# Running sums of the convolution taps of the third and fourth up stage in two free PSUM banks instead of SBUF

## The reference, cut to what matters

```python
def causal_dwconv(x, w, b=None):              # width 3 here
    y = sum(xp[:, j:j + t] * w[j] for j in range(width))
    return y if b is None else y + b

def conv_gated_mlp(hn, w_up, conv_w, conv_b, w_down):
    u = causal_dwconv(hn @ w_up, conv_w, conv_b)
    gate, val = jnp.split(u, 2, axis=-1)
    return (jax.nn.silu(gate) * val) @ w_down
```

## Time and profile before

| | us |
|---|---|
| three runs | 1355.68, 1353.02, 1345.2; median 1353.02 |
| the profiled execution | 1350.6, of which the span of the profile is 1348.8 |
| TensorE busy | 1277.2 (95%) |
| VectorE busy | 980.0 (73%) |
| ScalarE busy | 765.5 (57%) |
| GpSimd busy | 253.8 (19%) |

### The profile page before, as it was taken

The page is one execution under the profiler, slowest core; times in us unless marked ns, Lnnn a source line. Parts: engine busy times, 40 slices in busy tenths (PEclk is TensorE's granted clock), DMA queues, the critical chain, the costliest instruction groups (busy, mean ns, idle before and its releaser), DMA issues.

```text
span 1348.8 us, 28806 instructions
## 1 busy us (share of the span) xinstructions
PE 1277.2 (95%) x10587; PEld 1244.5 (92%) x10587; DVE 980.0 (73%) x1665; ACT 765.5 (57%) x1269; POOL 253.8 (19%) x233
## 2 busy tenths in 40 slices
PE   6999999999999999999968999999989998999997
PEld 6999999988999999988867999999989988999997
DVE  5766557876867755797799554789976786799954
ACT  5544445696554444579834554566665565666652
POOL 0000000010000000044406102345540021355500
PEclk9999999999999999999988999999999999999998
DMA  7555564563366656464527113865556523565563
GB/s 234 179 174 169 141 175 140 175 193 95 112 202 186 178 159 192 139 212 136 170 82 211 35 48 117 205 197 182 178 157 194 189 79 110 157 185 177 159 184 105
DMA packets 76733, 212.87 MB, mean 158 GB/s; under 512 B 7973, under 2 KB 22389, under 8 KB 76528
## 3 DMA queue, kind: packets, MB, share of 16 engines
q1 hardware_dynamic: 73536, 202.47, 49.3%
q0 software_dynamic: 2832, 9.04, 3.0%
q10 hardware_dynamic: 288, 0.33, 0.1%
HBM read 208.74 MB, written 3.06 MB: 157 GB/s over the span
## 4 chain that ended last, share of the span: by engine, by line
PE 61%; DVE 20%; issue 8%; DMA 4%; ACT 4%; POOL 2%; DVEq 1%; SPq 0%; ACTq 0%
PE bank L501 14%; PE bank L503 14%; PE bank L502 13%; DVE wl L394 4%; DVE cv L802 3%; DMA raw<-in_w_up 2%; DVE tp L782 2%; DVE cv L799 1%; PE bank L1549 1%; DVE sc L799 1%; DVE dVT L2219 1%; PE bank L2673 1%; PE bank L2763 1%; PE bank L1551 1%; DVE gTmp L2285 1%
## 5 line engine op out<-in xcount | busy, mean ns | idle before, releaser
L389 ACT ACTIVATE wh<-raw 128x1024 fp32r<-128x1024 f32 (+3 forms) x428 | 409.4, 963 | 312.3 <-PE bank L503 234.3
L394 DVE TENSOR_TENSOR wl<-raw,wh 128x1024 fp32r<-128x1024 f32 (+3 forms) x385 | 426.5, 1116 | 148.7 <-ACT wh L389 147.8
L501 PE MATMUL bank<-XH,wh 128*128 128x256 f32 (+1 forms) x1456 | 415.5, 285 | 13.5 <-DVE XL L890 7.0
L503 PE MATMUL bank<-XH,wl 128*128 128x256 f32 (+1 forms) x1456 | 413.0, 284 | 0.0
L502 PE MATMUL bank<-XL,wh 128*128 128x256 f32 (+1 forms) x1456 | 412.8, 284 | 0.0
L501 PEld LDWEIGHTS bank<-XH,wh 128*128 128x128 f32 x1456 | 275.6, 189 | 16.1 <-DVE XL L890 7.7
L503 PEld LDWEIGHTS bank<-XH,wl 128*128 128x128 f32 x1456 | 276.0, 190 | 0.0
L502 PEld LDWEIGHTS bank<-XL,wh 128*128 128x128 f32 x1456 | 274.7, 189 | 0.0
L501 PE MATMUL bank<-AH,wh 128*128 128x256 f32 (+1 forms) x704 | 199.0, 283 | 6.4 <-DVE wl L394 4.1
L394 POOL TENSOR_TENSOR wl<-raw,wh 128x1024 fp32r<-128x1024 f32 x43 | 113.3, 2637 | 480.0 <-ACT wh L389 479.8
L503 PE MATMUL bank<-AH,wl 128*128 128x256 f32 (+1 forms) x704 | 198.5, 282 | 0.0
(11 more groups left out here) (375 smaller groups left out, 2268.9 us busy)
## 6 DMA issues: line engine op xcount, KB each, us to landing
raw<-in_w_up SPq DMA_DIRECT2D x176, 512.0 KB, 4.3
raw<-in_w_down SPq DMA_DIRECT2D x64, 384.0 KB, 3.5
raw<-in_w_down SPq DMA_DIRECT2D x64, 320.0 KB, 3.1
raw<-in_w_gvz SPq DMA_DIRECT2D x32, 512.0 KB, 4.4
raw<-in_w_gqk SPq DMA_DIRECT2D x16, 512.0 KB, 5.1
raw<-in_w_gout SPq DMA_DIRECT2D x16, 512.0 KB, 4.5
raw<-in_w_mv SPq DMA_DIRECT2D x8, 512.0 KB, 5.0
raw<-in_w_mqk SPq DMA_DIRECT2D x8, 512.0 KB, 5.0
```

The costliest lines, as they stand in the source:

```text
L389: eng.activation(WH[s][:, 0:n, :], raw[s][:, 0:n, :], ACT.Copy).then_inc(s_hi[s], 1)
L394: eng.tensor_tensor(WL[s][:, 0:n, :], raw[s][:, 0:n, :], WH[s][:, 0:n, :].bitcast(F32), ALU.subtract).then_inc(s_lo[s], 1)
L501: eng.matmul(out, WH[s][:, i, :], xh, start=start, stop=False)
L503: mm = eng.matmul(out, WL[s][:, i, :], xh, start=False, stop=stop)
```

## The change

`tap2` and tap 1 write the running sum in a PSUM bank (bank 6 for even, bank 7 for odd units) and no longer in `dst`. Tap 0 reads the sum from the bank and writes the result to `dst` in SBUF, where `silu` and `prod` read it as before. The wait for the `silu` of the iteration before moves from ScalarE's `tap2` to VectorE's tap 0; for values a wait for the `prod` of the iteration before is added there. Both taps keep their numbers of elements, and no instruction is added or removed apart from the waits.

```diff
+            def sums(self, u):
+                return bank[6 + u % 2][:, 0:self.st.T]
+
             def tap2(self, eng, it, u):
                 m, T = it * 4 + u, self.st.T
                 evacuated(eng, self.st, it, u)
+                self.tap2s.done(eng.activation(self.sums(u), TP[u % 2][:, 3:3 + T], ACT.Identity,
+                                               bias=v(self.bias, m), scale=v(self.w, m + 88)), f"tap2_{u}")
+
+            def tap(self, eng, it, u):
+                m, T, acc = it * 4 + u, self.st.T, self.sums(u)
+                self.tap2s.wait(eng, it, f"tap2_{u}")
+                self.taps.done(eng.scalar_tensor_tensor(acc, TP[u % 2][:, 2:2 + T], v(self.w, m + 44), acc, ALU.mult,
+                                                        ALU.add), f"tap1_{u}")
+                self.taps.wait(eng, it, f"tap1_{u}")
                 if u % 2 == 0:
                     self.silus.wait(eng, it, f"silu{u // 2}", back=1)
-                self.tap2s.done(eng.activation(self.dst(u), TP[u % 2][:, 3:3 + T], ACT.Identity,
-                                               bias=v(self.bias, m), scale=v(self.w, m + 88)), f"tap2_{u}")
-
-            def tap(self, eng, it, u):
-                m, T, dst = it * 4 + u, self.st.T, self.dst(u)
-                self.tap2s.wait(eng, it, f"tap2_{u}")
-                self.taps.done(eng.scalar_tensor_tensor(dst, TP[u % 2][:, 2:2 + T], v(self.w, m + 44), dst, ALU.mult,
-                                                        ALU.add), f"tap1_{u}")
-                self.taps.wait(eng, it, f"tap1_{u}")
-                self.taps.done(eng.scalar_tensor_tensor(dst, TP[u % 2][:, 1:1 + T], v(self.w, m), dst, ALU.mult,
+                else:
+                    self.prods.wait(eng, it, f"prod{u // 2}", back=1)
+                self.taps.done(eng.scalar_tensor_tensor(self.dst(u), TP[u % 2][:, 1:1 + T], v(self.w, m), acc, ALU.mult,
                                                         ALU.add), f"tap0_{u}")
```

## The result

| | us |
|---|---|
| before, 14 runs | median 1351.63 (1342.14 to 1355.68) |
| after, 14 runs | median 1343.37 (1335.99 to 1349.8) |
| ratio after to before | 0.9945, 95% interval 0.9928 to 0.9963 |
| span of the profile | 1348.8 before, 1340.6 after |

The change makes the kernel 0.55% faster: 7.4 us by the ratio, 8.2 between the two spans. The forecast was 8.4.

A forecast was written before the change was run, and what follows sets the result against it. TensorE was taken to bound up4's middle and VectorE, by little, up3's. 1.5 + 2.59 + (2.52 - 0.1) + (2.07 - 0.1) = 8.5, taken as 8.4: 1353.0 - 8.4 = 1344.6 us, range 1337 to 1351.

The forecast's parts named there:

- Bounds: Middles of the up stages: VectorE bounds up3 by little, its period 0.16 us above TensorE's; TensorE bounds up4.
- Reading and writing PSUM: VectorE's taps: reading a bank is free, writing one taken as 0.48 us per tap, bounds 0.47 and 1.07.
- The exclusion: Taps with two SBUF inputs stand until GpSimd is done; with one, 2.40, 0.63 and 0.74 us fall to 0.48.
- VectorE per iteration: Up stage loop: 8.83 us of VectorE work, 9.2 with 0.1 for each wait, against TensorE's 11.37.
- Middle of up3: Up3's 33 units return to TensorE's pace, 95.25 to 93.75 us: 1.5 back.
- First gap: Between up3's last matmul and down3's first: the wait for VectorE's late `scale` goes, 2.59 us back.
- Second gaps: Fifth unit of down3 and down4, waiting for `WL`: 2.52 and 2.07 us lost, all but 0.1 each back.
- under 0.4 us in front of the fifth unit of each down stage: Sign expected in the profile after: TensorE's wait at the fifth unit of down3 and down4 stays below 0.4 us.
- (a): Rival, chance 0.14: table load and ScalarE's order keep both second gaps; 4.1 us gained, 1348.9.
- (b): Rival, chance 0.12: the 2.2 us stall for late weights from 880.50 to 888.90 goes too; 10.6 gained, 1342.4.
- (c): Rival, chance 0.05: the taps' `vec` column still counts as a second SBUF input; no gain, 1353.0.
- (d): Rival, chance 0.04: tap 1 updating a bank in place takes 1.07 us, VectorE's period becomes 11.6; slower, 1355.

The follow-up runs named there:

- e6: The kernel after with two useless taps more per unit on VectorE in up3 and up4; ratio to before 1.0233.
- e3: The kernel before, sums in SBUF, with all four low splits on VectorE in up3 and up4; ratio to before 0.9917.
- e5: The kernel after with one useless tap more per unit on VectorE in up3 and up4; ratio to before 0.9951.
- e10: The kernel after, GpSimd's copies for the attention waiting until TensorE finishes down3's fifth unit; run once, no ratio, second gap in down3 0.37 us.
- e7: The kernel before with the down stage's function table load moved in front of ScalarE's last `high` of up3 and up4; ratio to before 0.9983.
- e8: The kernel after with the down stage's function table load moved in front of ScalarE's last `high` of up3 and up4; ratio to before 0.9941.
- e11: The kernel after with the edits of e8 and e10, and GpSimd's eight bias loads moved behind up3; ratio to before 0.9997.
- e12: The kernel before with all four low splits on VectorE, early table load, late GpSimd copies and bias loads behind up3; ratio to before 0.9975.

## Why the prediction was right, and where its terms were off

- **Bounds.** VectorE by a hair in up3, TensorE in up4: right. Up3's 33 units went from 95.26 to 93.82 and up4's stayed at 93.72 in every run except e6.
- **Reading and writing PSUM.** 0.48 per tap taken, 479 to 480 ns measured, for tap 1 in place too. The Trainium skill's 125 ns on PSUM against 60 on SBUF for VectorE ("Perfetto Trace Analysis", "Optimizing Scalar/DVE Operations") shows neither in the read nor in the write. For ScalarE the same sentence gives 93 ns on SBUF and 51 on PSUM; there the trace agrees: `tap2` went from 601 to 556 ns when its output moved to PSUM.
- **The exclusion.** The rule of one SBUF input (the Trainium skill, "SBUF — State Buffer", "Who interferes with whom") held for 176 taps after, and both ways: GpSimd's own instructions got shorter, which the forecast had not counted. In the loop it needed no count, since GpSimd is not on the path there. The forecast did not see that the same rule costs time at the start of both stages, in `XL`, which the change leaves as it is (e3).
- **VectorE per iteration, 9.2 us.** In the iteration shown VectorE waits 1.9 of 11.36 us for TensorE, so it needs about 9.5. Four taps more fit (e5), eight don't (e6). The estimate of 0.1 for the waits was right in three of four units (0.23 to 0.26 instead of 0.14).
- **Middle of up3, 1.5:** 1.44. **First gap, 2.59:** 2.51 and 0.1 for the restart.
- **Second gaps, 0.1 left in each:** in down4 right, 0.01 and its restart. In down3 mis-sized: 0.81 stayed. From the last `scale` to `prod` it took 3.07 us in both, as forecast (3.06). The step that failed took up4's chain behind `prod`, 4.48 us from `prod` to TensorE, for both stages. In down3 the last link was already 0.45 longer before (the split of 1.41 next to GpSimd's copies, e10); a row of three splits in one, 3.00 us, hid it. The other 0.36 is the late last `scale` that some of the kernels have. So the sign "under 0.4 us in front of the fifth unit of each down stage" held in down4 and not in down3 (0.70). The loss of 0.7 was made up by 0.8 in the first 11 units and 0.1 before down4, which the sum had left out. The 0.8 has no cause in the change and lies within the scatter of these parts (34.6 to 37.8 in up3 and 38.7 to 40.2 in up4 among the kernels with GpSimd's split and the bias loads in their old place), so that the four stages come to 8.6 where the forecast had 8.4 is partly luck.
- **Rivals.** (a) The end staying, held by the table load: no, the change took 1.7 and 2.1 us off the second gaps. But the load was a link of the chain all along: moved alone it takes off 1.5 each (e7), and with both nothing is left (e8). (b) The stall at up3's start going too: no, it belonged to the bias loads (e11, e12). (c) The column of `vec` counting as a second input: no. (d) Slow updates in place: no.

What the forecast did not see is that the change is one of two cures. Giving GpSimd's low split back to VectorE, one line, has the same effect or a little more.

## What to carry to other kernels

An engine that is busy 94% of the time may be standing in its instructions: compare the same instruction's shortest and longest duration, and look at what GpSimd does during VectorE's long ones. Do so at the stages' starts and ends too: here the cured loop left the same stall in `XL`. The cure is to keep one of the two inputs in PSUM or to take the long instruction off GpSimd; either is worth only as much as the bounding engine waits for the late one, which the gaps between matmuls tell and busy shares don't. A transfer that disturbs one stage disturbs the next one if it is only moved; measure the stage that receives it.

## What the runs showed of the hardware that was not expected

- A VectorE split of 1.22 us stretched to 1.60 and 1.71 beside GpSimd (e6), and a GpSimd copy of one column from 0.18 to 0.91 beside a VectorE split (after): the exclusion hits small instructions as well as large ones, and in either direction.
- Behind a single idle time of TensorE its clock fell to 0.50 of full in e11 (3.49 us, ended at 1003.77; clock 0.50 from 1004.1 to 1007.5), in e12 (1.88 us, ended at 995.83; 0.50 from 996.7 to 1000.1) and in e6 (2.90 us, ended at 1000.65; 0.50 from 1001.5 to 1004.9). The two gaps of 2.5 us in the kernel before, 7.8 us of matmuls apart, did not do that, so the length of a gap alone does not decide it. This is the window of before from the end of up3 on, clock 1.00:

```profile
983.98:1049.00 65.02, 60.42 (x511) 60.09 (x510) 45.10 (x71) 38.12 (x63) 10.82 (x23) 1.00 0.62 183
```

- The last `scale` of up3 started 0.36 us later in five of ten kernels, those in which VectorE's up stages are the same to the instruction, with no wait shown. Open.
